# Behind the experts: last sums, first low parts, squares and weight sums on GpSimd, all evictions of turned tiles on ScalarE

## The reference, cut to what matters

```python
f = hier_moe(x, ...)                                    # sum over a token's two experts
x = layer_norm(ALPHA * x + f, ln_g[layer, 1], ln_b[layer, 1])
...
h = rmsnorm(x, g_ffn1[l])                               # x * rsqrt(mean(x*x) + EPS) * g
x = x + 0.5 * swiglu(h, w1_a[l], w3_a[l], w2_a[l])      # (silu(h @ w1) * (h @ w3)) @ w2
```

## Time and profile before

| what | value |
|---|---|
| median of 3 runs | 2808.46 us (2802.94 to 2809.16) |
| the profiled execution's own time | 2803.92 us |
| its span, first to last instruction | 2801.9 us |
| mean granted TensorE clock | 0.991 of full |
| busy: TensorE, VectorE, ScalarE, GpSimd | 97%, 63%, 39%, 15% of the span |

### The profile page before, as it was taken

How to read it: one execution, slowest core, us unless ns; L and a number is a source line. 1 busy time by engine, 2 the same in 40 slices (tenths; PEclk the granted TensorE clock), 3 DMA queues, 4 the chain that set the end, 5 groups by cost and what they waited for, 6 DMA issues and landing times.

```text
span 2801.9 us, 40254 instructions
## 1 busy us (share of the span) xinstructions
PE 2716.1 (97%) x15816; PEld 2181.3 (78%) x15816; DVE 1774.7 (63%) x2645; ACT 1092.5 (39%) x1586; POOL 416.2 (15%) x464
## 2 busy tenths in 40 slices
PE   9998999889699999999999999999999999999998
PEld 6576343333399998888889999899998888899997
DVE  6635232222787776665588777986777655787775
ACT  6832110100454444332354444554444233354443
POOL 3211000000021111101131110311101111221111
PEclk9999999999899999999999999999999999999999
DMA  5146999999465643332345564456542333365651
GB/s 214 45 175 263 420 420 420 420 420 421 141 181 166 173 136 100 103 101 94 100 124 168 167 172 136 114 164 176 158 136 89 94 94 106 98 172 142 176 158 60
DMA packets 138176, 505.65 MB, mean 180 GB/s; under 512 B 17025, under 2 KB 17537, under 8 KB 113153
## 3 DMA queue, kind: packets, MB, share of 16 engines
q1 hardware_dynamic: 101952, 422.36, 40.4%
q0 software_dynamic: 34688, 73.42, 12.8%
q10 hardware_dynamic: 1344, 7.23, 0.6%
HBM read 502.95 MB, written 4.19 MB: 181 GB/s over the span
## 4 chain that ended last, share of the span: by engine, by line
PE 73%; DMA 14%; DVE 5%; issue 4%; ACT 2%; POOL 1%; SPq 0%; DVEq 0%; ACTq 0%; POOLq 0%
PE bank L658 22%; PE bank L656 22%; PE bank L657 22%; DMA raw_more<-in_moe 4%; DMA raw<-in_moe 3%; PE bank L804 3%; DMA raw_over<-in_moe 3%; PE bank L839 2%; DVE w_lo L1875 1%; DMA sums<-in_w_b 1%; ACT w_hi L1272 1%; PE bank L662 1%; DMA raw<-in_w_b 1%; DVE ft L2289 0%; DMA x_rows<-x_tok 0%
## 5 line engine op out<-in xcount | busy, mean ns | idle before, releaser
L1875 DVE TENSOR_TENSOR w_lo<-raw,w_hi 128x1024 fp32r<-128x1024 f32 (+1 forms) x346 | 434.6, 1269 | 272.2 <-ACT w_hi L1272 265.7
L656 PE MATMUL bank<-xf_hi,w_lo 128*128 128x256 f32 x2112 | 590.1, 279 | 17.2 <-DVE w_lo L1875 9.6
L658 PE MATMUL bank<-xf_hi,w_hi 128*128 128x256 f32 x2112 | 585.3, 277 | 0.0
L657 PE MATMUL bank<-xf_lo,w_hi 128*128 128x256 f32 x2112 | 585.2, 277 | 0.0
L1272 ACT ACTIVATE w_hi<-raw 128x1024 fp32r<-128x1024 f32 (+1 forms) x356 | 366.0, 1039 | 273.9 <-PE bank L658 247.3
L656 PEld LDWEIGHTS bank<-xf_hi,w_lo 128*128 128x128 f32 x2112 | 397.6, 188 | 27.2 <-issue 14.1
L657 PEld LDWEIGHTS bank<-xf_lo,w_hi 128*128 128x128 f32 x2112 | 397.6, 188 | 2.4 <-issue 1.0
L658 PEld LDWEIGHTS bank<-xf_hi,w_hi 128*128 128x128 f32 x2112 | 397.4, 188 | 0.0
L658 PE MATMUL bank<-g_hi,w_hi 128*128 128x512 f32 x832 | 327.4, 394 | 0.0
L657 PE MATMUL bank<-g_lo,w_hi 128*128 128x512 f32 x832 | 326.2, 392 | 0.0
L656 PE MATMUL bank<-g_hi,w_lo 128*128 128x512 f32 x832 | 323.5, 389 | 0.3 <-DVE g_lo L2331 0.3
(11 more groups left out here) (367 smaller groups left out, 4549.0 us busy)
## 6 DMA issues: line engine op xcount, KB each, us to landing
raw_more<-in_moe SPq DMA_DIRECT2D x96, 1024.0 KB, 26.5
raw_over<-in_moe SPq DMA_DIRECT2D x48, 1024.0 KB, 27.4
raw<-in_w_a SPq DMA_DIRECT2D x77, 512.0 KB, 6.1
raw<-in_w_b SPq DMA_DIRECT2D x76, 512.0 KB, 6.3
raw<-in_w_in SPq DMA_DIRECT2D x73, 512.0 KB, 3.6
raw_top<-in_moe SPq DMA_DIRECT2D x24, 1024.0 KB, 27.9
raw<-in_moe SPq DMA_DIRECT2D x24, 1024.0 KB, 28.6
sums<-in_w_a POOLq DMA_DIRECT2D x88, 256.0 KB, 4.9
```

The costliest lines, as they stand in the source:

```text
L656: e.matmul(out, a_lo, b_hi, start=start, stop=False, skip_group_check=partial)
L657: e.matmul(out, a_hi, b_lo, start=False, stop=False, skip_group_check=partial)
L658: return e.matmul(out, a_hi, b_hi, start=False, stop=stop, skip_group_check=partial)
L1875: e.tensor_tensor(lo, source_of(k), hi.bitcast(F32), ALU.subtract).then_inc(s["lo"], 1)
```

## The change

It touches only the stretch between the last expert pair and the first up pair. VectorE sums the last pair's outputs for token tiles 0 and 1; for 2 and 3 ScalarE copies the banks to `xe` (`cbc`) and GpSimd adds them to `x_tok` (`cbp`). GpSimd makes the low parts of the first four blocks of the feed-forward (`AB` and `S` of pair 0), the eight squares of the first norm and the first two weight sums. ScalarE evicts all eight turned tiles, no longer squares them, and makes the high parts of S inside round k = 2. TensorE turns seven tiles of each token tile at once and has the sums of squares behind the products. GpSimd's branch stands behind the first two low parts.

```diff
--- before.py
+++ after.py
@@ -281,9 +281,10 @@
         if n < NPAIR:
             use(("ht", n), "htc", n + 1, 2)
     for i in range(2 * TT):
-        use(("cb", NPAIR - 1, i), "cba", 2 * TT * (NPAIR - 1) + i + 1, (0, 1, 4, 2, 3, 7, 5, 6)[i])
+        use(("cb", NPAIR - 1, i), *(("cba", 2 * TT * (NPAIR - 1) + i + 1) if i < TT else ("cbc", i - TT + 1)),
+            (0, 1, 4, 2, 3, 7, 5, 6)[i])
     for n in range(DT):
-        use(("fin", n), "ftd" if n % 2 else "fta", n // 2 + 1, (0, 1, 4, 5, 2, 3, 6, 2)[n])
+        use(("fin", n), "fta", n + 1, (0, 1, 4, 5, 2, 3, 6, 2)[n])
     for l in range(LAYERS):
         for i in (2 * l, 2 * l + 1):
             for j in range(UP):
...
@@ -545,10 +546,10 @@
             return s["used"], in_used[c + 1]
 
         def on_pool(c):
-            return c < N_REC and c % 3 == 2
+            return c % 3 == 2 if c < N_REC else c <= at["S", 0, 0, 1]
 
         def lo_signal(c):
-            n = sum(on_pool(k) for k in range(min(c + 1, N_REC)))
+            n = sum(on_pool(k) for k in range(min(c, at["S", 0, 0, 1]) + 1))
             return (s["lo_pool"], n) if on_pool(c) else (s["lo"], c + 1 - n)
 
         def expert_done(name, e, v):
@@ -871,7 +872,8 @@
             combine(NPAIR - 1, 0, 2 * TT)
 
             with e.If(more != 0):
-                e.wait_ge(s["cba"], 2 * TT * NPAIR)
+                e.wait_ge(s["cba"], 2 * TT * NPAIR - TT)
+                e.wait_ge(s["cbc"], TT)
                 for x in range(EXTRA):
                     e.wait_ge(s["b_rows"], 16 * (x + 1))
                     if x >= 1:
@@ -921,12 +923,11 @@
 
             for tt in range(TT - 1):
                 e.wait_ge(s["xn2"], tt + 1)
-                for n in (0, 1, 2, 4):
+                for n in range(DT - 1):
                     turned(n, [tt])
-            turned(5, range(TT - 1))
             e.wait_ge(s["xnv"], 1)
             for n in range(DT - 1):
-                turned(n, range(TT) if n in (3, 6) else [TT - 1])
+                turned(n, [TT - 1])
 
             def square_sum(n):
 
@@ -977,18 +978,18 @@
 
                     xs = [free_bank(("X", 0, m)) for m in range(2)]
                     product(0, xs, 0)
-                    square_sum(0)
-                    square_sum(1)
                     product(0, xs, 1)
                     ys = [free_bank(("Y", 0, m)) for m in range(2)]
                     product(1, ys, 0)
                     product(1, ys, 1)
                     turned(DT - 1, range(TT))
+                    square_sum(0)
+                    square_sum(1)
                     for k in (2, 3):
+                        product(0, xs, k)
+                        product(1, ys, k)
                         square_sum(2 * k - 2)
                         square_sum(2 * k - 1)
-                        product(0, xs, k)
-                        product(1, ys, k)
                 for m in range(2 if n else 0):
                     hi, lo = weights(("AB", i, j, m))
                     xs[m] = free_bank(("X", n, m))
@@ -1434,7 +1435,12 @@
             e.wait_ge(s["cntok"], 1)
             more = e.value_load(cnt[0:1, 0:1], min_val=0, max_val=EXTRA)
             e.wait_ge(s["mu"], UNITS)
-            high(at["AB", 0, 0, 1])
+            high(at["AB", 0, 0, 0])
+            e.wait_ge(s["xtn"], 2 * NPAIR)
+            for q in range(TT):
+                e.wait_ge(s["cbm"], 2 * TT * (NPAIR - 1) + TT + q + 1)
+                e.activation(xe[:, q // 2, q % 2 * T:q % 2 * T + T], bank_of(("cb", NPAIR - 1, TT + q))[:, :], ACT.Copy) \
+                    .then_inc(s["cbc"], 1)
             for tt in range(TT + 1):
                 if tt < TT:
                     e.wait_ge(s["stt"], 4 * TT + 4 * tt + 4)
@@ -1444,6 +1450,8 @@
                     e.wait_ge(s["srec"], TT + 2 * a + 2)
                     e.activation(x_n[:, a, :], x_tok[:, a, :], ACT.Identity, scale=st[:, a, 16:17], bias=st[:, a, 17:18]) \
                         .then_inc(s["xn2"], 1)
+                    if a == 0:
+                        high(at["AB", 0, 0, 1])
 
             with e.If(more != 0):
                 for x in range(EXTRA):
@@ -1500,14 +1508,32 @@
                 e.activation(xf_hi[:, k, 5 * HALF:7 * HALF], t[:, 3, :], ACT.Copy).then_inc(s["xgh"], 1)
                 square(p, n)
 
-            for n, j in enumerate(TILES):
-                if n % 2 == 0:
+            def stream(n):
+                if n < DT:
+                    j = TILES[n]
                     e.wait_ge(s["fin"], n + 1)
                     e.activation(xT[:, j, :], bank_of(("fin", n))[:, :], ACT.Identity,
                                  scale=par("ln_g", DT + j), bias=par("ln_b", DT + j)).then_inc(s["fta"], 1)
-                if n >= 1:
-                    finish(0, n - 1, "fta" if n % 2 else "ftd", (n - 1) // 2 + 1)
-            finish(0, DT - 1, "ftd", DT // 2)
+
+            def first_high(k, form, of, width):
+                t = ft[:, k % 2, :, :].rearrange("p a n -> p (a n)")
+                e.wait_ge(s["xgf"], 6 * k + (1, 3, 5, 6)[of])
+                e.activation(xf_hi[:, k, form * HALF:form * HALF + width], t[:, of * T:of * T + width], ACT.Copy,
+                             scale=1.0 if of else -1.0).then_inc(s["xgh"], 1)
+
+            stream(0)
+            stream(1)
+            for k in range(KH):
+                first_high(k, 0, 0, HALF)
+                stream(2 * k + 2)
+                first_high(k, 1, 1, T)
+                stream(2 * k + 3)
+                if k == 2:
+                    high(at["S", 0, 0, 0])
+                first_high(k, 3, 2, T)
+                first_high(k, 5, 3, T)
+                if k == 2:
+                    high(at["S", 0, 0, 1])
 
             def root(p):
                 e.wait_ge(s["rs1"], p + 1)
@@ -1754,8 +1780,24 @@
             more = e.value_load(cnt[0:1, 0:1], min_val=0, max_val=EXTRA)
             gather(NPAIR - 1)
 
+            e.wait_ge(s["cba"], 2 * TT * (NPAIR - 1))
+            for q in range(TT):
+                x = x_tok[:, TT // 2 + q // 2, q % 2 * T:q % 2 * T + T]
+                e.wait_ge(s["cbc"], q + 1)
+                e.tensor_tensor(x, x, xe[:, q // 2, q % 2 * T:q % 2 * T + T], ALU.add).then_inc(s["cbp"], 1)
+
+            def first_low(key):
+                c = at[key]
+                hi, lo = split_of(c)
+                e.wait_ge(s["hi"], c + 1)
+                e.tensor_tensor(lo, source_of(c), hi.bitcast(F32), ALU.subtract).then_inc(s["lo_pool"], 1)
+
+            first_low(("AB", 0, 0, 0))
+            first_low(("AB", 0, 0, 1))
+
             with e.If(more != 0):
                 e.wait_ge(s["mu"], UNITS)
+                e.wait_ge(s["cbp"], TT)
                 e.memset(o_raw, 0.0).then_inc(s["rows"], 1)
                 e.wait_ge(s["rows"], TT + 2)
                 for x in range(EXTRA):
@@ -1782,24 +1824,67 @@
 
             def weight_sums(i, j):
 
+                weight_loads(i, j)
+                weight_adds(i, j)
+                mixed_adds(i, j)
+
+            def raised(i, j):
+                return [io[f"{w}_{'ab'[i % 2]}"][i // 2, j + UP] for w in ("w1", "w3")]
+
+            def weight_loads(i, j):
                 n = UP * i + j
-                high = [io[f"{w}_{'ab'[i % 2]}"][i // 2, j + UP] for w in ("w1", "w3")]
+                high = raised(i, j)
                 for m in range(2):
                     if n >= 1:
                         k = at["S", (n - 1) // UP, (n - 1) % UP, m]
                         e.wait_ge(*lo_signal(k))
                         e.wait_ge(s["wsum"], 4 * (n - 1) + 3 + m)
                     e.dma_start(sums[:, m, 0:T], high[m][:, 0:T]).then_inc(s_sum[m], 16)
+
+            def weight_adds(i, j):
+                n = UP * i + j
+                high = raised(i, j)
                 for m in range(2):
                     e.wait_ge(s_sum[m], 32 * n + 16)
                     e.dma_start(sums[:, m, 0:T], high[m][:, T:W], accum_op=ALU.add).then_inc(s_sum[m], 16)
+
+            def mixed_adds(i, j):
+                high = raised(i, j)
                 for m in range(2):
                     r = load_at["up", i, j, m, 1]
                     e.wait_ge(s_raw[slot[r]], landed[r])
                     e.dma_start(up_raw(i, j, m, 1)[:, 0:T], high[m][:, 0:T], accum_op=ALU.add).then_inc(s_sum[2 + m], 16)
 
+            def first_square(n):
+                j = TILES[n]
+                e.wait_ge(s["fta"], n + 1)
+                if n >= 3:
+                    e.wait_ge(s["acc"], n - 2)
+                e.tensor_tensor(sq[:, n % 2, :] if n else rsq[:, :], xT[:, j, :], xT[:, j, :], ALU.mult) \
+                    .then_inc(s["sqr"], 1)
+
+            def first_sum(m):
+                r = load_at["up", 0, 0, m, 0]
+                e.wait_ge(s_raw[slot[r]], landed[r])
+                e.wait_ge(s_sum[m], 32)
+                e.tensor_tensor(sums[:, m, T:W], sums[:, m, 0:T], up_raw(0, 0, m, 0)[:, 0:T], ALU.add).then_inc(s["wsum"], 1)
+
             e.wait_ge(s["mu"], UNITS)
-            weight_sums(0, 0)
```

(37 more changed lines are left out.)

4 lines of the change are left out of this document (2 added, 2 removed).

## The result

| what | before | after |
|---|---|---|
| median (lowest to highest) of the runs taken together, 8 each | 2805.79 us (2801.26 to 2809.16) | 2813.07 us (2808.99 to 2814.11) |
| ratio, 95% interval | | 1.0027 (1.0018 to 1.0037) |
| span of the profiled execution | 2801.9 us | 2811.0 us |
| first form-4 product (S), behind ScalarE's first high part of the last expert pair | 48.1 us | 57.2 us |
| from S to the last instruction | 2031.8 us | 2030.8 us |

What follows compares the result with a forecast made beforehand. TensorE, 97% busy, bounds except in a gap set by VectorE. Rounds from 741.1 plus 19.3 plus 12.6 end at 773.0; S 6.6 us late, 1.4 given back: net 5.2, rounded 5, slower, 2813.5 us; range 2803 to 2821.

Steps and rivals of the forecast that it cites:

- What bounds, and S: Gap before the first up pair: VectorE's chain sets the first form-4 product; moving it moves the end by as much.
- Tail: Experts' sums, statistics, normalization: 128x1 step waits 1.7 us for GpSimd; first eviction at 740.3 for 742.44, 2.1 us gained.
- its bounds: Limiting cases for the whole time: no exclusion 2804.1 us, half clock throughout 2819.4; 128x1 step free, 1.1 less.
- Evictions: ScalarE takes all eight turned tiles; VectorE's rounds take 4.82 us each, four 19.3 without new waits.
- Squares, sums and lows: GpSimd's operations in VectorE's four rounds: its reads and ScalarE's wait for weight sum 0 add 12.6 us.
- rival 3: TensorE stays at 1.2 GHz through the rounds: 8 to 11 us lost, 2816.5 to 2819.4; chance 0.19.
- signs of being wrong: Rounds of 4.8 us throughout, first form-4 product before 770, or clock 0.50 until 756 and again behind that product.
- Up to S: From last low part to first form-4 product, 773.0 to 776.7: 6.6 us late, 1.4 given back by full clock.
- similar idle: TensorE nearly still from 760.5 to 769.6; a like idle before had left its clock at 0.50 from 770.0 to 773.4.
- Free help: GpSimd's operations run beside VectorE's in the rounds: 4.4 us gained, 2804, up to 9; chance 0.20.
- Even: Contention as forecast, but 128x1 step free and TensorE keeps its clock over the gap: 1 to 4 us lost; chance 0.15.

Runs made afterwards that it cites:

- kernel 6: Changed kernel with GpSimd's six weight DMA starts moved ahead of VectorE's rounds; 2809.4 us in one execution.
- kernel 1: Kernel before the change, plus twelve GpSimd products of a spare tile that nothing uses, started from the first eviction; 2817.0 us in one execution.
- kernel 4: Changed kernel with the squares back on ScalarE and their sums on TensorE in the order of before; 2803.1 us in one execution.
- kernel 5: Changed kernel with the two low parts of S made by VectorE again, behind the rounds; 2809.8 us in one execution.
- kernel 7: kernel 6 once more, unchanged; 2810.8 us over 7 runs.

## Why the prediction was right, and where its terms were off

*What bounds, and S.* Right. S came 9.1 us later (57.2 against 48.1), the stretch behind it was 1.0 shorter, and the rest reached the end; the table shows the same for the experiments, as closely as single executions can.

*Tail.* Right: first eviction 741.26 - 1.02 = 740.24, forecast 740.3. The one step that no row of before showed, whether a 128x1 operation waits, came out as taken: 1.80 instead of 0.16. The prediction prices that wait at 1.7, at 2.0 (gain 4.1 for 2.1) and, in its bounds, at 1.1; by these rows it is 1.6. By the Trainium skill, "SBUF — State Buffer", section "Who interferes with whom", it had to, and the trace agrees. Rounds start at 741.05, forecast 741.1.

*Evictions.* Right: rounds 1 and 3 take 4.88 and 4.84, forecast 4.82.

*Squares, sums and lows,* per round beyond 4.82:

| | forecast | measured |
|---|---|---|
| round 0 | 2.2 | 3.7 |
| round 1 | 0.2 | 0.1 |
| round 2, VectorE waiting for ScalarE | 3.9 | 6.1 |
| round 2, VectorE standing behind reads | 3.5 | 6.0 |
| round 3 | 2.8 | 0.0 |
| sum | 12.6 | 15.9 |

Round 0 was mis-sized because I gave the two accumulating DMA starts their 0.90 each on GpSimd and nothing on VectorE: they held a gain product for 1.4 us more, which kernel 6 gave back. The reads in rounds 2 and 3 have nearly the right sum, 6.0 against 6.3, but not the place: I let a waiting engine get every other turn, so that square 5 and low S1 would fall into round 3, and GpSimd, with its next operation always taken up ahead, kept VectorE out for all four. The wait for the first weight sum was 2.2 too small. GpSimd's square 3 began 4.0 behind the start of round 2 and not 2.5, since TensorE was at half clock until some 757.6: its products end later by 0.5 than I had them, four turns took 0.85 (756.04 to 756.89) instead of 0.5, the sums of squares some 2.3 instead of 1.9 (0.3 of the 1.5 I can't place). The other 0.7 is that VectorE's second low part would have come 3.6 behind the start of the round without any wait, where I had put it at 4.4. So rival 3, the slow clock, had part of the truth in two rounds of four, and its price of 8 to 11 us is where the spans ended (9.1). One of the prediction's signs of being wrong came with it: the clock was at 0.50 until some 757.6, and again from 773.8 until 782, 1.8 past S. But the terms that hang on it come to some 2 us of the 9.1, and kernels 1, 4 and 5 show that the reads make most of the rest.

*Up to S.* S came 2.9 behind the last low part (780.20 - 777.27), forecast 3.7; its record is 1.20 long where 0.55 is usual at this clock, so some of the 0.8 is where a record begins and not time. The two sums of squares (four matmuls) before it cost the 3.4 forecast (3.62 with their overlap). Behind S 1.4 was to be given back by a full clock. The first S products still ran at half clock, until 782, though TensorE had worked since 773.87; the prediction had them at the full one. The "similar idle" that it draws on was 3.14 us (before 770.08), where TensorE now stood still for 11.4. From S to the next sums of squares it took 4.06 (780.20 to 784.26) instead of 4.42 (770.08 to 774.50), so the rows show 0.4 given back there. The whole stretch behind S is 1.0 shorter, but kernels 6 and 7, one kernel, differ by 0.8 in it. The balance: 5.2 forecast, 3.3 more in the rounds, 0.8 less up to S, 0.4 less given back (taking the 1.0): 8.1, which is the 9.1 of the spans less the 1.02 of the untouched start.

*The rivals.* Free help falls by kernel 1. Even (the 128x1 step free, TensorE at its clock over the gap) falls by both its conditions: 1.80, and 0.50 from 773.8.

## What to carry to other kernels

An idle GpSimd is no free helper for a VectorE that runs two-input operations on SBUF or products with a column: each of its reading operations stops VectorE, and a DMA start can stop a product, so its work belongs where VectorE waits for another engine. There a smaller offload, the four additions and the two low parts of AB, was part of kernels that were 0.27% faster instead of 0.27% slower; ScalarE's evictions and earlier weight sums had their share in that, and no run parts them in time. Look at how tightly GpSimd's instructions follow each other as well: several ready reads in a row can hold a waiting VectorE for all of them, and one wait between two of them opened the gap here. And when a step is moved to an engine, follow who waits for what stands behind it there: here a square's buffer made ScalarE wait for a weight sum.
